# Dilated heads: order of ScalarE's copies and of TensorE's transposes, and a second buffer for squares

## The reference, cut to what matters

```python
def dilated_mixer(cols, cos, sin, q_gain, k_gain):
    B, S, _ = cols.shape
    qkv = cols.reshape(B, S, 3, N_GROUPS_2, A_HEADS, HEAD_DIM)
    q = rms_norm(qkv[:, :, 0], q_gain[:, None, :])
    k = rms_norm(qkv[:, :, 1], k_gain[:, None, :])
    v = qkv[:, :, 2]
    ...
    q = apply_partial_rotary(q, cos5, sin5)
    k = apply_partial_rotary(k, cos5, sin5)
    for g, (window, dil) in enumerate(DIL_PAIRS):
        o, lse = dilated_window_attention(q[:, :, g], k[:, :, g], v[:, :, g], dil, window // dil)
        ...
    alpha = jax.nn.softmax(jnp.stack(lses, axis=0), axis=0)
    o = jnp.sum(alpha[..., None] * jnp.stack(outs, axis=0), axis=0)
```

## Time and profile before

| | us |
|---|---|
| median of three timed runs | 2127.6 |
| lowest and highest | 2125.8, 2128.46 |
| the profiled execution | 2122.27 |
| its span, first to last instruction | 2120.5 |
| the dilated stage in it, about | 935 to 1530 |

### The profile page before, as it was taken

The page is one execution under the profiler, slowest core; times in us unless marked ns, Lnnn a source line. Parts: engine busy times, 40 slices in busy tenths (PEclk is TensorE's granted clock), DMA queues, the critical chain, the costliest instruction groups (busy, mean ns, idle before and its releaser), DMA issues.

```text
span 2120.5 us, 27981 instructions
## 1 busy us (share of the span) xinstructions
PE 1988.5 (94%) x10551; PEld 1686.9 (80%) x10551; DVE 1164.7 (55%) x2292; ACT 1038.3 (49%) x1704; POOL 306.3 (14%) x418
## 2 busy tenths in 40 slices
PE   7999999999899999999999999999999989998999
PEld 7977667677777777788888988988778777877887
DVE  3344377553899998744443444434443535747562
ACT  4644433344687877654443444344333555345441
POOL 0601132010000011201220121112010001302210
PEclk9999999999999999999999999999999999999999
DMA  4411122126699999512222222222242511121120
GB/s 144 135 50 40 60 60 70 31 95 248 222 354 366 349 368 359 174 48 75 68 68 68 68 61 68 72 64 89 80 138 90 164 45 60 51 60 60 60 100 40
DMA packets 178016, 255.57 MB, mean 121 GB/s; under 512 B 13565, under 2 KB 92234, under 8 KB 177882
## 3 DMA queue, kind: packets, MB, share of 16 engines
q1 hardware_dynamic: 168832, 221.33, 32.3%
q0 software_dynamic: 8784, 31.92, 4.0%
q10 hardware_dynamic: 266, 0.52, 0.1%
HBM read 239.57 MB, written 14.16 MB: 120 GB/s over the span
## 4 chain that ended last, share of the span: by engine, by line
PE 79%; DVE 8%; ACT 6%; issue 3%; DMA 3%; POOL 1%; ACTq 0%; SPq 0%; DVEq 0%; POOLq 0%
PE pb L2328 51%; PE pb L2692 6%; PE pb L2356 6%; PE pb L2715 3%; DVE wlo L1534 3%; PE pb L2913 3%; ACT whi L937 2%; PE pb L2833 2%; PE pb L2412 2%; PE pb L2822 2%; PE pb L2425 2%; DMA wraw<-w_down 1%; PE pb L2579 1%; ACT arena L972 1%; PE pb L2932 1%
## 5 line engine op out<-in xcount | busy, mean ns | idle before, releaser
L2328 PE MATMUL pb<-whi,AT_hi 128*128 128x512 f32 (+4 forms) x1992 | 771.0, 387 | 30.0 <-DVE arena L2125 6.7
L1534 DVE TENSOR_TENSOR wlo<-wraw,whi 128x1024 fp32r<-128x1024 f32 (+4 forms) x430 | 490.7, 1150 | 527.4 <-ACT whi L937 519.1
L2328 PE MATMUL pb<-whi,AT_lo 128*128 128x512 f32 (+4 forms) x1992 | 728.5, 366 | 0.0
L2328 PE MATMUL pb<-wlo,AT_hi 128*128 128x512 f32 (+4 forms) x1992 | 726.4, 365 | 0.0
L937 ACT ACTIVATE whi<-wraw 128x1024 fp32r<-128x1024 f32 (+4 forms) x446 | 440.5, 992 | 415.6 <-PE pb L2328 353.1
L2328 PEld LDWEIGHTS pb<-whi,AT_hi 128*128 128x128 f32 x1992 | 377.4, 189 | 106.6 <-issue 46.5
L2328 PEld LDWEIGHTS pb<-whi,AT_lo 128*128 128x128 f32 x1992 | 376.3, 189 | 45.6
L2328 PEld LDWEIGHTS pb<-wlo,AT_hi 128*128 128x128 f32 x1992 | 378.1, 190 | 38.2 <-issue 2.9
L2356 PE MATMUL pb<-arena 128*128 128x128 f32 (+1 forms) x1180 | 180.3, 280 | 52.8 <-ACT arena L972 30.6
L2356 PEld LDWEIGHTS pb<-arena 128*128 128x128 f32 (+1 forms) x1180 | 144.4, 146 | 92.1 <-ACT arena L972 39.7
L2692 PE MATMUL pb<-whi,AT_hi 128*128 128x512 f32 x256 | 104.0, 406 | 2.0 <-DVE AT_lo L1952 2.0
(11 more groups left out here) (310 smaller groups left out, 2344.7 us busy)
## 6 DMA issues: line engine op xcount, KB each, us to landing
wraw<-w_in_a SPq DMA_DIRECT2D x288, 128.0 KB
wraw<-w_gate SPq DMA_DIRECT2D x128, 256.0 KB
wraw<-w_up SPq DMA_DIRECT2D x128, 256.0 KB
wraw<-w_down SPq DMA_DIRECT2D x58, 512.0 KB
wraw<-w_in_b SPq DMA_DIRECT2D x40, 512.0 KB
wraw<-w_in SPq DMA_DIRECT2D x28, 512.0 KB
wraw<-w_mem_kv SPq DMA_DIRECT2D x16, 512.0 KB
wraw<-w_in_a SPq DMA_DIRECT2D x16, 512.0 KB
```

Of the source, the lines that this page charges most:

```text
L1534: dve.tensor_tensor(w_slot(wlo, p, p % SPL), raw_slot(p), w_slot(whi, p, p % SPL).bitcast(F32), ALU.subtract).then_inc(lo_done[p % SPL], 1)
L2328: mm = pe.matmul(ACC[t][:, 0:n], a, b, start=kc == 0 and q == 0, stop=i == c["count"] - 1 and kk == per - 1 and q == 2)
```

## The change

Three edits. On TensorE the pair of groups 0 and 1 moves from behind tile 2 to behind tile 1, with its wait for the rope; group 2 stays behind tile 3. On ScalarE the copies of groups 0 and 1 move ahead of the split of that step; the copy of group 2 stays behind it. The squares go in turn to two buffers, `sqb` and the first half of `rtmp`, and the square of tile t waits for the sum of tile t - 2.

```diff
-        sqb = take(384)
+        sqs = [take(384), rtmp[:, 0:384]]
...
-                                if t or n:
-                                    act.wait_ge(S("qk_red"), NT * n + t)
-                                act.activation(sqb, ACC[t][:, 0:384], ACT.Square, scale=rs_perm[:, t:t + 1]).then_inc(S("qk_sq"), 1)
+                                if t >= 2 or n:
+                                    act.wait_ge(S("qk_red"), NT * n + t - 1)
+                                act.activation(sqs[t % 2], ACC[t][:, 0:384], ACT.Square, scale=rs_perm[:, t:t + 1]).then_inc(S("qk_sq"), 1)
+                    name, dst = (f"dq_{hd}", qT) if i == 6 else (f"dk_{hd}", kT)
+                    if i in (6, 10):
+                        for g in (0, 1):
+                            tcopy(name, g, dst[:, hd % 2, g, :], tb(name, g))
                     if n or nm == "v" or q == 3:
                         feed(chunks[j]["first"] + q + SPL)
...
                     if i in (6, 10):
-                        name, dst = (f"dq_{hd}", qT) if i == 6 else (f"dk_{hd}", kT)
-                        for g in range(3):
-                            tcopy(name, g, dst[:, hd % 2, g, :], tb(name, g))
+                        tcopy(name, 2, dst[:, hd % 2, 2, :], tb(name, 2))
...
-                            dve.tensor_reduce(qk_n["ss"][:, 3 * t:3 * t + 3], sqb.rearrange("p (g c) -> p g c", g=3), AX.X, ALU.add
+                            dve.tensor_reduce(qk_n["ss"][:, 3 * t:3 * t + 3], sqs[t % 2].rearrange("p (g c) -> p g c", g=3), AX.X, ALU.add
...
-                            if t == 2:
+                            if t == 1:
                                 pe.wait_ge(S("qk_rot"), 2 * hd + (i == 10) + 1)
-                            for g in ((), (), (0, 1), (2,))[t]:
+                            for g in ((), (0, 1), (), (2,))[t]:
```

## The result

| | before | after |
|---|---|---|
| median, us | 2127.41 (4 runs, 2125.8 to 2128.46) | 2098.61 (4 runs, 2094.17 to 2101.77) |
| ratio | | 0.9864, 95% interval 0.9845 to 0.9883 |
| the profiled execution's span, us | 2120.5 | 2097.5 |

The change makes the kernel 28.8 us faster in the median; 2100.6 was predicted. The two profiled executions differ by only 23.0 us, and that has to be understood first. I cut each into three by instructions that both have: the last sixteen matmuls of the memory attention (936.92 before, 935.00 after) and the scores of the last turn (1483.96 and 1454.12). The views are the stretches of the kernel after (length, busy time of PE, PEld, DVE, ACT and POOL with counts, granted clock, DMA share, GB/s), and behind them the third stretch of the kernel before.

A forecast was written before the change was run, and what follows sets the result against it. TensorE's own stream was taken to bound the kernel. Copies and pair (23.0 us) plus squares (4.0) gave 27.0 us, taken off the median 2127.6: 2100.6 us, range 2096 to 2110.

The forecast's parts named there:

- queries, a head: Query site, heads 1 to 7: projection resumes 1.32 us sooner because the third copy starts when the split ends.
- keys, a head: Key site, heads 1 to 7: the third group's 1.64 us wait goes, less 0.1 us for VectorE's copies.
- squares, a head: Behind the queries, eight heads: two steps between tiles 0.27 us shorter each, so tile 3's bank comes 0.5 us sooner.
- head 0, all parts: Head 0: 1.65 us gained at the queries, 1.3 at the keys and 0.5 from the squares.
- A head 68.5 us in place of 71.9: Sign in the changed trace: length of one dilated head; staying above 70 us would show the prediction wrong.
- The wait was read from starts, 1.65 us: Query site, head 3: third group's transposes could start at 1165.57 but start at 1167.22, waiting for ScalarE's first copy.
- What is late next: Query site: third copy stays behind the split, still delaying the next unit's last two transposes; it starts at 1166.59, not 1167.91.
- The 0.1 us for VectorE's copies: Key site, heads 1 to 7: the earlier pair waits 0.1 us for banks VectorE empties; bounds 0 and 1.5 us.
- Rival (a): Key site, heads 1 to 7: port lock delays VectorE's copies up to 1.5 us; 17 us gained, 2111 us; chance 0.10.
- Groups two tiles apart: Query and key sites: first two groups go one tile (1.04 us) sooner, credited together with the copies ahead; 23.0 us.
- A wait of some 0.5 us for the rope: Head 0's keys: the earlier pair would wait 1.2 us for GpSimd's rope, but part 2 brings it about 0.7 forward.
- the banks of tiles 1 and 2: Behind the queries: they come a little sooner than TensorE asks, so only tile 3's wait was counted, 0.5 us a head.

The follow-up runs named there:

- part 2 alone: Only the second buffer of squares added to the kernel before, transposes and copies as before; median 2122.42 us beside 2125.43, ratio 0.9992.
- kernel with all three edits: Changed kernel with the pair behind tile 2, the queries' third copy ahead of the split, probabilities copied behind tile 3; 2088.01 us, ratio 0.9821.

## Why the prediction was right

It was right in time (2100.6 for 2098.61), and term by term:

| term | forecast | measured |
|---|---|---|
| queries, a head | 1.32 | 1.34 (19.30 - 17.96) |
| keys, a head | 1.54 | 1.60 (18.86 - 17.26) |
| squares, a head | 0.5 | 0.55 (17.61 - 17.06, part 2 alone) |
| head 0, all parts | 3.45 | 3.53 (45.41 - 41.88) |
| sum | 27.0 | 27.9 |

The sum is seven heads and head 0; 0.3 us more in head 3 and 0.3 less in head 7 cancel. "A head 68.5 us in place of 71.9" was head 3's: a usual one went from 71.6 to 68.1.

**Copies ahead of the split.** The wait was read from starts, 1.65 us, and not from the idle time of the waits view (1.48): that is what made the size right. "What is late next" was named too, the third copy behind the split, and it is most of the 0.61 us that is left: with it ahead of the split too, 0.26 us remain (1.8 us in seven places).

**The pair at the keys.** The 0.1 us for VectorE's copies was shown by leaving the move out: 17.15 against 17.26. In the changed kernel VectorE's copies start at 1171.41:

```profile
1171.41 1.02 DVE L2085 COPY arena<-pb 128x512 f32<-128x512 f32 x2
```

The first lasts 0.69 us, so to 1172.10, and the pair follows at 1172.25, that is 0.83 us behind the start of the copies. It is 0.83 us in all seven heads, head 7 too, where the copies are later, and in the kernel with the pair moved alone; in the kernel before, where nothing waits, it was 1.8 us (1.3 in head 7). No experiment of its own moved these copies, and the list of waits names them in head 7 of some kernels only, but a lag that is the same at 14 places leaves little else. Rival (a), that the shared port makes these copies late by up to 1.5 us, did not come about: seven heads show 0.1 us.

**Groups two tiles apart.** Here the prediction put the gain to the edit as a whole ("now go in one tile sooner") and asked only whether the copies end in time, not by how much. With its own rows it could have been seen: a copy starts 0.69 us after its transposes (1167.22 to 1167.91), so with the pair behind tile 2 both copies are done by 1165.4, before the third group asks at 1165.57. The move was not needed and costs 0.1 us in each head and some 0.7 us in head 0 (41.9 against 41.1 above). This does not change the sum, since these costs were in it, but it is a wrong share of credit.

**Head 0.** A wait of some 0.5 us for the rope was forecast and 0.57 measured; without the second buffer 1.2, as worked out.

**The squares.** 0.5 us, 0.55 measured, but not all at the place that was named. VectorE's steps between tiles went from 0.79 to 0.52 us, in head 3 of the kernel after:

```profile
1134.70 0.61 DVE L2127 SCALAR_TENSOR_TENSOR arena<-pb,small,arena 128x384 f32<-128x384 f32 x1
1135.22 0.54 DVE L2125 TENSOR_REDUCE small<-arena 128x3 f32<-128x384 f32 x1
```

The prediction said that the banks of tiles 1 and 2 come a little sooner than TensorE asks, and that tile 3 waits 0.5 us less. No row stood for the first, and it was wrong. These are the first matmuls of tiles 1, 2 and 3 behind the queries of head 2, in the kernel before and in the kernel after; tile 0 starts at 1076.30 and at 1067.36:

```profile
1077.46 0.45 PE L2328 MATMUL pb<-whi,AT_hi 128*128 128x384 f32 x1
...
1078.72 0.44 PE L2328 MATMUL pb<-whi,AT_hi 128*128 128x384 f32 x1
...
1080.70 0.45 PE L2328 MATMUL pb<-whi,AT_hi 128*128 128x384 f32 x1 [0.64 <-DVE arena L2125]
```

```profile
1068.48 0.33 PE L2330 MATMUL pb<-whi,AT_hi 128*128 128x384 f32 x1
...
1069.52 0.33 PE L2330 MATMUL pb<-whi,AT_hi 128*128 128x384 f32 x1
...
1071.21 0.44 PE L2330 MATMUL pb<-whi,AT_hi 128*128 128x384 f32 x1 [0.49 <-DVE arena L2127]
```

From tile to tile it took 1.16, 1.26 and 1.98 us before and takes 1.12, 1.04 and 1.69 now. So 0.26 of the 0.55 us were lost at tiles 1 and 2, in waits too short for the list, and only 0.29 went at tile 3. The sum was right because tile 3's bank is the end of VectorE's chain wherever TensorE waits on the way.

**From one execution to the median.** I took the 5.3 us between the profiled execution and the median as a constant. It is not one: it goes with the clock. The profiled execution of before was a lucky one (mean granted clock 0.992, where 23 executions of that kernel have a median of 0.988) and that of after was not (0.987), so their difference understates the gain by 4.9 us. The forecast came out because the gain was taken off the median.

## What to carry to other kernels

When an engine in order has both a long job without a near reader and short ones that free a buffer, put the short ones first if they are ready in time; the gain, once for each place where the other engine stands, is all the time from its turn to the end of the short job: here 1.65 us, twice the split's own 0.84, since the first copy stood in the wait as well. Ask of each edit alone whether it is needed: here one of two edits to the order brought all of it and the other cost a little. And measure a stage from an instruction to an instruction in the trace: lengths of the same steps agreed within 0.05 us from head to head and kernel to kernel, save in heads 3 and 7 and under a lower clock, while whole executions of one kernel differed by up to 17 us.

## What the runs showed of the hardware

The time of an execution goes with its granted clock. The kernel with all three edits took 2083.12 us at a mean granted clock of 0.991 and 2100.27 at 0.983; the kernel before took, on one chip, 2119.80 at 0.992 and 2134.13 at 0.983. That is 2.1 and 1.6 us for each thousandth. The falls are short. Some are in every one of the ten traces, near 205, 490 and 550 us; others are in one trace and not in the other. In the kernel after, stretches of 4 us in the last layer, and in the kernel before the same instructions 29.84 us later:

```profile
1832.16:1836.16 4.00, 3.12 (x26) 2.85 (x26) 3.35 (x9) 3.15 (x4) 2.08 (x3) 1.00 0.00 0
1836.16:1840.16 4.00, 3.22 (x11) 2.32 (x12) 3.09 (x5) 2.28 (x5) 0.00 (x0) 0.51 0.45 128
1840.16:1844.16 4.00, 3.31 (x16) 3.10 (x16) 0.86 (x2) 0.60 (x1) 0.00 (x0) 0.64 0.02 7
```

```profile
1862.00:1866.00 4.00, 3.12 (x25) 2.85 (x25) 3.35 (x9) 3.26 (x4) 1.99 (x3) 1.00 0.00 0
1866.00:1870.00 4.00, 3.21 (x24) 2.72 (x23) 3.85 (x6) 2.18 (x5) 0.00 (x0) 1.00 0.49 134
1870.00:1874.00 4.00, 3.31 (x16) 2.61 (x15) 0.00 (x0) 0.60 (x1) 0.00 (x0) 1.00 0.00 1
```

Up to the fall both are alike: TensorE is busy 3.12 of 4 us. Then one execution gets the lower level for some 7 us (0.51 over 4 us, then 0.64 over 4) and gets through 11 matmuls in the first 4 us where the other does 24. With this fall and two more that the other does not have (at 1901 and 1925), the 29.84 us between the two executions shrink to the 23.0 of the whole spans. So a short idle time is no certain loss but a chance of one: in the part 2 trace it was drawn twice in seven heads, in the trace of before in none. The gap ahead of the fall at 1094 was 1.48 us idle, with a second short wait behind it. Whether removing the waits also makes such falls rarer is open: the three traces with the wait at the queries have two falls at its 21 places in heads 1 to 7, the seven traces without it none at 49, which is too few to tell.
